# A transformer and delta-rule kernel on one core: program loops written out, and as loops of the engines

## The reference

```python
for l in range(DEPTH):                       # DEPTH = 2
    h = rms_norm(x, norm_g[l])
    proj = h @ w_in[l]
    (pool_u, pool_z, aq, ak, av, az, iq, ik, iw, mq, mz, gates) = jnp.split(proj, split_points, axis=-1)
    y_pool = multi_scale_pool(pool_u, ...) * silu(pool_z)
    y_attn = dsa_attention(...) * silu(az)
    y_mem  = memory_attention(...) * silu(mz)
    merged = g0 * (y_pool @ w_branch[l, 0]) + g1 * (y_attn @ w_branch[l, 1]) + g2 * (y_mem @ w_branch[l, 2])
    x = x + merged @ w_out[l]
```

## Time and profile before

| | us |
|---|---|
| median of three runs (1484.16 to 1487.32) | 1484.87 |
| the profiled execution | 1487.32 |
| its span, first to last instruction | 1485.5 |
| TensorE busy | 1334.9 (90%) |
| VectorE busy | 858.3 (58%) |
| ScalarE busy | 633.5 (43%) |
| GpSimd busy | 263.6 (18%) |
| mean granted TensorE clock, share of full | 0.947 |

### The profile page before, as it was taken

One profiled execution on the slowest core, in us unless ns is written; L12 is line 12 of the kernel. 1 busy time (PEld: TensorE's weight loads), 2 busy tenths in 40 slices (PEclk: granted clock), 3 DMA queues, 4 the chain that ended last, 5 costly groups with the idle time before them and its releaser, 6 DMA issues.

```text
span 1485.5 us, 28707 instructions
## 1 busy us (share of the span) xinstructions
PE 1334.9 (90%) x12138; PEld 1271.9 (86%) x12138; DVE 858.3 (58%) x1352; ACT 633.5 (43%) x1040; POOL 263.6 (18%) x259
## 2 busy tenths in 40 slices
PE   4889989989899989999658789999999899799997
PEld 3879988889799978899558789989999799799997
DVE  4334744556536645655488967667656565555554
ACT  5424544443434434433434653333333363544443
POOL 0000040006000130143042226235334000000000
PEclk9989998999899989999889999999999899899999
DMA  4625452335434533344323432222222255355553
GB/s 175 203 79 171 155 186 86 128 111 173 136 129 150 191 114 114 114 162 151 97 85 100 128 114 79 80 91 72 83 83 77 88 182 166 122 190 182 194 189 125
DMA packets 59119, 195.13 MB, mean 131 GB/s; under 512 B 6248, under 2 KB 13928, under 8 KB 58736
## 3 DMA queue, kind: packets, MB, share of 16 engines
q1 hardware_dynamic: 49248, 179.33, 37.1%
q10 hardware_dynamic: 9440, 12.90, 2.6%
q0 software_dynamic: 304, 1.07, 0.3%
HBM read 189.06 MB, written 4.21 MB: 130 GB/s over the span
## 4 chain that ended last, share of the span: by engine, by line
PE 78%; DVE 11%; ACT 4%; issue 2%; DVEq 1%; POOL 1%; DMA 1%; POOLq 1%; ACTq 0%
PE stream_ps L278 21%; PE stream_ps L280 20%; PE stream_ps L279 20%; DVE w_lo L270 4%; DVE qkvT L1100 2%; PE free_ps L1640 2%; PE free_ps L1657 1%; ACT w_hi L264 1%; PE free_ps L356 1%; PE free_ps L1658 1%; DVEq L1106 1%; PE free_ps L1405 1%; DVE bcv L1147 1%; DMA cst<-cst_dram 1%; PE free_ps L1363 1%
## 5 line engine op out<-in xcount | busy, mean ns | idle before, releaser
L278 PE MATMUL stream_ps<-h_hi,w_hi 128*128 128x256 f32 (+1 forms) x2016 | 598.4, 297 | 55.5 <-DVE w_lo L270 26.3
L270 DVE TENSOR_TENSOR w_lo<-raw,w_hi 128x1024 fp32r<-128x1024 f32 x342 | 431.1, 1267 | 334.1 <-ACT w_hi L264 331.2
L279 PE MATMUL stream_ps<-h_lo,w_hi 128*128 128x256 f32 (+1 forms) x2016 | 583.5, 289 | 0.0
L280 PE MATMUL stream_ps<-h_hi,w_lo 128*128 128x256 f32 (+1 forms) x2016 | 583.1, 289 | 0.0
L278 PEld LDWEIGHTS stream_ps<-h_hi,w_hi 128*128 128x128 f32 x2016 | 396.1, 196 | 65.9 <-issue 34.2
L280 PEld LDWEIGHTS stream_ps<-h_hi,w_lo 128*128 128x128 f32 x2016 | 396.2, 197 | 0.0
L279 PEld LDWEIGHTS stream_ps<-h_lo,w_hi 128*128 128x128 f32 x2016 | 395.1, 196 | 0.4 <-issue 0.2
L264 ACT ACTIVATE w_hi<-raw 128x1024 fp32r<-128x1024 f32 x342 | 358.3, 1053 | 58.1 <-PE stream_ps L280 52.4
L1224 DVE TENSOR_TENSOR xy<-xy,free_ps 64x128 f32<-64x128 f32 x180 | 44.7, 283 | 65.0 <-PE free_ps L1658 50.8
L1100 DVE SCALAR_TENSOR_TENSOR qkvT<-st_raw,gains,qkvT 128x272 f32<-128x272 f32 x96 | 65.7, 726 | 5.3 <-ACT qkvT L682 2.6
L795 ACT ACTIVATE n<-free_ps 64x128 f32<-64x128 f32 x80 | 22.0, 275 | 106.2 <-PE free_ps L1640 105.3
(11 more groups left out here) (327 smaller groups left out, 2097.7 us busy)
## 6 DMA issues: line engine op xcount, KB each, us to landing
raw<-stream_dram SPq DMA_DIRECT2D x342, 512.0 KB, 3.3
gate_spill<-gate_out ACTq DMA_DIRECT2D x16, 128.0 KB, 2.1
xT<-xT_dram ACTq DMA_DIRECT2D x1, 1088.0 KB, 10.0
stage<-wik_dram ACTq DMA_DIRECT2D x2, 544.0 KB, 4.1
mem_raw<-memT_dram ACTq DMA_DIRECT2D x1, 1024.0 KB, 6.5
hankel<-rel_scratch POOLq DMA_DIRECT2D x1, 1024.0 KB, 10.3
x_spill<-xT ACTq DMA_DIRECT2D x1, 1024.0 KB, 4.8
gb<-gate_spill ACTq DMA_DIRECT2D x1, 1024.0 KB, 5.6
```

The source lines that it names most:

```text
L270: nc.vector.tensor_tensor(w_lo[s][:, :, :], raw[:, s, :].rearrange("p (k n) -> p k n", k=KT), w_hi[s][:, :, :].bitcast(F32), ALU.subtract) ...
L278: nc.tensor.matmul(ps, l_hi, r_hi, start=first, stop=False)
L279: nc.tensor.matmul(ps, l_hi, r_lo, start=False, stop=False)
L280: return nc.tensor.matmul(ps, l_lo, r_hi, start=False, stop=last)
```

## The change

In 35 places `for x in range(a, b)` becomes `with engine.Fori(a, b) as x`. The body is then in the program once, and the engine runs it with a register as loop variable; it counts up, compares and branches back. The bodies and the helper functions are unchanged, and what each engine computes, waits for and issues stays in the same order. Not all loops change: those with a fixed small body (`for s in range(SLOTS)`), the first loops over the memory and the norms' loops stay written out, and the fifth step of the delta rule stays outside its loop as before.

```diff
@@ -372,7 +372,7 @@   SyncE: the stream, 85 turns of four transfers
-            for G in range(0, a["groups"]):
+            with sp.Fori(0, a["groups"]) as G:
                 for s in range(SLOTS):
                     sp.wait_ge(lo_ready, 4 * G + s + 1)
@@ -550,7 +550,7 @@   ScalarE: the layer loop (the same on GpSimd, VectorE, TensorE)
-            for l in range(0, LAYERS):
+            with act.Fori(0, LAYERS) as l:
                 G = G0 + LAYER_GROUPS * l
@@ -594,7 +594,7 @@   ScalarE: pairs of heads inside it (and mp, br, w; the same on the others)
-                for hp in range(0, 4):
+                with act.Fori(0, 4) as hp:
                     for s in range(SLOTS):
                         ahead(split_hi, act, G + 9 + hp, s)
@@ -805,7 +805,7 @@   ScalarE: the delta rule's first four steps (GpSimd: all five, line 477)
-            for t in range(0, GATE_STEPS):
+            with act.Fori(0, GATE_STEPS) as t:
                 step(t, True)
             step(GATE_STEPS, False)
@@ -859,7 +859,7 @@   ScalarE: gate and up
-            for w in range(0, FT // 2):
+            with act.Fori(0, FT // 2) as w:
                 for s in range(SLOTS):
                     ahead(split_hi, act, G_GU + w, s)
                     if s % 2 == 0:
@@ -1304,7 +1304,7 @@   VectorE: gate and up
-            for w in range(0, FT // 2):
+            with dve.Fori(0, FT // 2) as w:
@@ -1389,11 +1389,11 @@   TensorE: five groups in the layer, then pairs of heads
-                for g in range(0, 5):
+                with pe.Fori(0, 5) as g:
-                for hp in range(0, 4):
+                with pe.Fori(0, 4) as hp:
@@ -1685,7 +1685,7 @@   TensorE: the delta rule's first four steps
-            for t in range(0, GATE_STEPS):
+            with pe.Fori(0, GATE_STEPS) as t:
                 step(t, True)
@@ -1711,11 +1711,11 @@   TensorE: gate and up, turns 1 to 10, and down
-            for w in range(1, FT // 2):
+            with pe.Fori(1, FT // 2) as w:
                 for s in range(SLOTS):
                     block_cols(pe, G_GU + w, s, dve_evac, D2 + 40 + 4 * w + s + 1, hS_hi, hS_lo)
             pe.wait_ge(flo_ready, FT)
-            for w in range(0, 2):
+            with pe.Fori(0, 2) as w:
```

More of the change, by code:

```diff
@@ L426, in _ @@
                     nc.gpsimd.tensor_copy(st_v, v[:, :, bass.ds(hp * P, P)]).then_inc(v_staged, 1)
-                for mp in range(0, 2):
+                with pool.Fori(0, 2) as mp:
                     pool.wait_ge(pv_done, 6 * l + 4 + mp + 1)
@@ L434, in _ @@
                 nc.gpsimd.drain()
-                for br in range(0, 3):
+                with pool.Fori(0, 3) as br:
                     for s in range(SLOTS):
@@ L476, in _ @@
                 nc.gpsimd.memset(buffer[:, :, :, :], 0.0)
-            for t in range(0, STEPS):
+            with pool.Fori(0, STEPS) as t:
                 nc.gpsimd.drain()
@@ L613, in _ @@
                             op.then_inc(softT_ready, 1)
-                for mp in range(0, 2):
+                with act.Fori(0, 2) as mp:
                     for s in range(SLOTS):
@@ L631, in _ @@
                             op.then_inc(softT_ready, 1)
-                for br in range(0, 3):
+                with act.Fori(0, 3) as br:
                     for s in range(SLOTS):
@@ L840, in _ @@
             act.dma_start(xS, a["x_spill"][:, :, tok]).then_inc(x_back, 16)
-            for w in range(2, 4):
+            with act.Fori(2, 4) as w:
                 for s in range(SLOTS):
@@ L849, in squares @@
             def squares(G, D_at):
-                for w in range(0, 2):
+                with act.Fori(0, 2) as w:
                     for s in range(SLOTS):
@@ L914, in _ @@
             dve.wait_ge(admit_in, 16)
-            for l in range(0, LAYERS):
+            with dve.Fori(0, LAYERS) as l:
                 G = G0 + LAYER_GROUPS * l
@@ L976, in split_y @@
                     return nc.vector.tensor_tensor(dst_lo, src, dst_hi.bitcast(F32), ALU.subtract)
-                for hp in range(0, 4):
+                with dve.Fori(0, 4) as hp:
                     for s in range(SLOTS):
@@ L1013, in _ @@
                 nc.vector.drain()
-                for mp in range(0, 2):
+                with dve.Fori(0, 2) as mp:
                     for s in range(SLOTS):
@@ L1032, in _ @@
                     nc.vector.drain()
-                for br in range(0, 3):
+                with dve.Fori(0, 3) as br:
                     for s in range(SLOTS):
@@ L1047, in _ @@
                                                    in1=hS_hi[:, ks, :].bitcast(F32), op0=ALU.mult, op1=ALU.subtract).then_inc(mlo_ready, 1)
-                for w in range(0, 2):
+                with dve.Fori(0, 2) as w:
                     for s in range(SLOTS):
@@ L1351, in _ @@
             pe.wait_ge(ident_ready, 1)
-            for l in range(0, LAYERS):
+            with pe.Fori(0, LAYERS) as l:
                 G = G0 + LAYER_GROUPS * l
@@ L1430, in _ @@
                 mm.then_inc(mixed_done, 1)
-                for mp in range(0, 2):
+                with pe.Fori(0, 2) as mp:
                     pe.wait_ge(qk_staged, 6 * l + 4 + mp + 1)
@@ L1457, in _ @@
                     mm.then_inc(pv_done, 1)
-                for br in range(0, 3):
+                with pe.Fori(0, 3) as br:
                     pe.wait_ge(act_evac, SLOTS + E + ACT_EVACS)
```

8 lines of the change are left out of this document (4 added, 4 removed).

## The result

Changed kernel 1507.26 us (median, 1505.96 to 1510.24), kernel before in the same session 1486.09 (1484.16 to 1489.71): ratio 1.0142, 95% interval 1.0116 to 1.0169. The profiled execution took 1507.09 us, with a span of 1505.3, for 1487.32 and 1485.5 before.

A forecast was written before the change was run, and what follows sets the result against it. The prediction took TensorE, busy 90% of the span and nearly full in gate/up and the steps, as the bound. Terms 5 + 3 + 2 + 3 = +13 us on the 1484.87 us median gave 1498 us, range 1485 to 1528.

The forecast's parts named there:

- the first case: Whole kernel: the summed terms hold, 1498 us, own range 1489 to 1510; chance 0.55.
- Table loads in gate/up, +5: Gate/up loop: two ScalarE table loads a turn plus register work overdraw the ring's slack, +5 us (0 to 16).
- Branches at the step's end, +3: Step loop on TensorE: three branches back miss their target, 1 us of 2.5 uncovered each, +3 us (0 to 10).
- Register work in the steps, +2: Recurrence steps: register instructions behind a wait, at VectorE's lines 1184 and 1242, +2 us (0 to 8).
- The rest, +3 (0 to 8): Layer edge, norm stages and edges next to TensorE's waits for pv_used: together +3 us (0 to 8).
- Head pairs, 0: Head-pair loop: table load before the first split costs 0; otherwise 0.5 us at each of 6 added loads.
- Second rival, every edge fetches: TensorE's 35 branches back each miss, about 3.3 us, 1 uncovered in block loops; +45 us, 1530; chance 0.20.
- Fourth rival, faster for fewer pages: TensorE's code: loops that sit in the window avoid late instruction pages, -5 us at most, 1480; chance 0.07.
- The signs: Expected in the trace: 56 table loads, gate/up turns of 11.8 to 12.0 us, three 1 us gaps at step ends.

The follow-up runs named there:

- e4: The changed kernel with the gate/up loop written out on ScalarE alone: 1506.94 us.
- e7: The kernel before with only the gate/up loops of ScalarE, VectorE and TensorE as hardware loops: 1489.59 us median, ratio 0.9997.
- e11: The changed kernel with mp and gate/up loops written out on ScalarE, VectorE and TensorE, and the layer loop on TensorE: 1519.75 us.
- e8: The kernel before with only the four mp loops as hardware loops: 1486.32 us, ratio 1.0002.
- e6: The kernel before with only the four step loops as hardware loops: 1486.51 us, ratio 0.9996.
- run 387: Not a follow-up run: 387 counts VectorE's register instructions of 69 ns in the median, in the whole run of the changed kernel.
- e2: The changed kernel with GpSimd clearing merged only once VectorE has written y_lo of the first mp turn: 1502.28 us.
- e1: The changed kernel with the mp loops written out on TensorE, ScalarE and VectorE: 1495.7 us.
- e3: The changed kernel with the layer loop written out on TensorE alone: 1501.01 us.
- e12: The kernel before with TensorE's wait for y before branch br at 4 + br of the layer's six turns, not all six: 1480.71 us, ratio 0.9969.
- e9: The kernel before with the layer loops of four engines, and GpSimd's loops inside its own, as hardware loops: 1487.86 us, ratio 1.0006.
- e10: The kernel before with layer loops of four engines, GpSimd's inner loops and the other three engines' mp loops as hardware loops: 1493.26 us.

## Why the prediction was right, and where its steps were not

The time lies within its range and in the first case's own (1489 to 1510), 9 us above the forecast. The sum was +13 and the spans differ by 19.8, but the terms are not those that made it: of the 10 us given to gate/up and the steps about 3 came, and some 21 came where the last term allowed 0 to 8. Spells at 1.2 GHz that moved elsewhere took some 4 back. That these errors left the time in the range is in good part luck.

- *Table loads in gate/up, +5.* The term was mis-sized. 56 loads came, as forecast, but a turn took 11.48 us on VectorE (the starts of its branches, 1313.2 to 1428.0 in ten turns), for 11.36 before and 11.86 forecast. ScalarE's timeline, for the earlier trace rows:

```profile
1365.61 0.42 ACT L870 ACTIVATE f_hi<-f_val 128x256 f32 x1 [1.73 <-DVE f_val L1313]
...
1366.89 0.36 ACT L867 ACTIVATE f_act<-stream_ps 128x256 f32<-128x256 f32 x1
...
1369.93 0.42 ACT L870 ACTIVATE f_hi<-f_val 128x256 f32 x1 [1.73 <-DVE f_val L1313]
1370.36 1.28 ACT L264 ACT_TABLE_LOAD   x1
1371.66 1.06 ACT L264 ACTIVATE w_hi<-raw 128x1024 fp32r<-128x1024 f32 x1
1372.73 1.28 ACT L867 ACT_TABLE_LOAD   x1
1374.03 0.39 ACT L867 ACTIVATE f_act<-stream_ps 128x256 f32<-128x256 f32 x1
```

A half turn without loads takes 4.32 us, not the 4.42 that the earlier trace rows gave without its two waits, since f_act now needs no wait and overlaps w_hi; and the 0.2 of register work a turn isn't on the ring. 0.1 in each half and 0.2 of register work are the 0.4 between 11.86 and 11.48. Eleven overdrafts of 0.12 are the 1.3 us of e4; they appear where TensorE waits for f_lo at the exit (2.7 us for 1.5), and behind it comes a spell of 3.4 us at 1.2 GHz (1.6 us), as in e7. The spell came in e4 and e11 too, behind waits of 2.0 and 1.8 us, and in e8 not, behind 1.8.
- *Branches at the step's end, +3.* Nothing, here and in e6: the targets were loaded. The gap of 1 us three times is not there.
- *Register work in the steps, +2.* Nothing either: stretch 320.0 us for 320.4. VectorE's register instructions (in the whole run 387 of 69 ns in the median and 414 of 40) lie in its waits there.
- *The rest, +3 (0 to 8).* This is the step that failed, with 20.9 us in place of 3 and far over its upper bound: "the layer edge, the norm stages, the edges next to TensorE's waits for pv_used" came to 5.5 at the edge, 1.1 at the end of layer 1 and 7.2 and 7.1 in the mp loops. The edge is the branch, 4.50 us against the 2.5 I had taken for a miss and had charged to the steps, and the spell behind it. The mp loops are a chain (L1027, copy, y_lo, w_lo, maxima) without slack on VectorE, where 0.5 us of delay met another engine's clearing and grew to 2.7, and the longer waits brought on spells at 1.2 GHz. Of the 7.2 us in layer 0, 3.3 are these spells, 1.7 the collision itself (after against e2) and the rest, 2.2, register work and its waits: with the mp loops undone (e1) 1.3 stay.
- *Head pairs, 0.* Holds: no loss there.
- *Second rival, every edge fetches.* 34 of 35 did not. The Trainium skill (Runtime: NRT & Kernel Launch, "Instruction fetch mechanics") lets a branch out of a two-page window stall. The same section of the Trainium skill gives TensorE a larger instruction memory than the others, 128 KiB, which is eight of its 16 KiB pages. The trace disagrees with two pages and agrees with eight: the step loop's 1,773 instructions stay, and the layer loop, of 2,385 recorded ones with each inner body counted once, does not. The prediction took the two pages and left out the eight. But e11 shows how near it was: the step loop alone, behind other code, costs 28 us.
- *Fourth rival, faster for fewer pages.* The packets halved (97 to 52) and nothing came of it.
- *The signs.* The 56 loads came. The turn of 11.8 to 12.0 us and the gaps of 1 us at the steps' ends did not; the sign for loops that stay loaded, fewer packets and no gaps at the edges, came at all edges but one.
- *What was not in the prediction at all:* the granted clock. A wait that grows may bring a spell of 3.4 us at 1.2 GHz behind it, 1.6 us more. Of the 7.1 us of an mp loop, 3.3 are this (after against e3), of the edge's 5.5 and of gate/up's 3.3, 1.6 each.

## What to carry to other kernels

A hardware loop is nearly free where its body stays loaded and its engine waits anyway (e6, e8), and it costs 4 to 5 us a turn where it doesn't, and as much again in e11 by the clock; which of the two holds changed in e11 with code far ahead of the loop, so read the longest branch of each loop line in the trace after every edit, also after one elsewhere. Look for the loss on short chains between two engines, where some tenths of a microsecond can put an instruction beside another engine's long write, rather than in the sum of added instructions. Where a wait covers more than its reader reads, splitting it (e12) won 4.4 us of the median, more than a kind of loop cost in any of e6 to e9.

## What the hardware showed that I had not expected

- A taken compare-and-branch took 0.21 us on TensorE in the median, at most 0.26 (0.076 not taken) and 0.056 on VectorE, 0.045 on ScalarE, GpSimd and SyncE; with the target not loaded 4.06 to 4.98 us on TensorE, in the seven kernels that had such a branch (after, e1, e2, e4, e9 and e10 at the layer's edge, e11 in the steps).
- A 128x512 copy of VectorE took 0.43 us alone (e2). Where it overlapped a GpSimd instruction in the first mp turn, it ended 0.28 us after that instruction, in both layers of the other thirteen kernels: behind the 128x512 copy L431 it took 0.59 to 0.82 by how early in L431 it began, with the 128x2048 clearing 2.14 (after, e3, e4). It was so although its recorded start was 0.05 to 0.07 us ahead of the clearing's. The subtraction y_lo of the same size took 0.69 us beside the clearing (before, at 317.88 us) and without it (e2): not every VectorE instruction is held.
- In before, after and e1 to e12 TensorE's 1.2 GHz came in spells of 3.4 to 13.7 us. Most began at or soon after a gap of TensorE of a microsecond or more, some in the head pairs behind one of 0.6 to 0.7 us, and some behind none (at 105.6 us before). Nearly the same gaps drew 3.4 us at 1.2 GHz in one kernel and 10.2 in another (the mp loop of e3 and after).
